# GpSimd's preparation of RWKV's first pass in pieces that wait for VectorE's units, and the two scans at the in-projection's end

## The reference, cut to what matters

```python
def block(q_blk):
    s = jnp.einsum('bhcqd,bhckd->bhcqk', q_blk, kt).astype(f32)
    pr = jax.nn.softmax(s, axis=-1)
    pd = pr[:, :, 0] - lam * pr[:, :, 1]
    return jnp.einsum('bhqk,bhkv->bhqv', pd.astype(vt.dtype), vt)
```

```python
w_log = -jax.nn.softplus(-(w0 + jnp.einsum('bsdr,drc->bsdc', jnp.tanh(wd), w2))) - 0.5
decay = jnp.exp(-jnp.exp(w_log))
a = jax.nn.sigmoid(a0 + jnp.einsum('bsdr,drc->bsdc', ad, a2))
kk = kk / jnp.maximum(jnp.sqrt(jnp.sum(kk * kk, axis=-1, keepdims=True)), 1e-12)
k_dir = k * (1.0 + (a - 1.0) * k_a)
```

## Time and profile before

| | |
|---|---|
| median of 3 runs | 1949.75 us (1945.37 to 1950.09) |
| the profiled execution | 1950.11 us, span 1948.4 us |
| busy: TensorE / VectorE / ScalarE / GpSimd | 95% / 57% / 36% / 11% |
| mean granted TensorE clock | 0.984 of full speed |
| last tile of the in-projection taken out | 1092.41 |
| VectorE's first reduction of the attention | 1097.02 |
| VectorE's first instruction of RWKV's heads | 1153.37 |

### The profile page before, as it was taken

One profiled execution on the slowest core, in us unless ns is written; L12 is line 12 of the kernel. 1 busy time (PEld: TensorE's weight loads), 2 busy tenths in 40 slices (PEclk: granted clock), 3 DMA queues, 4 the chain that ended last, 5 costly groups with the idle time before them and its releaser, 6 DMA issues. The chain is left out here.

```text
span 1948.4 us, 35667 instructions
## 1 busy us (share of the span) xinstructions
PE 1860.3 (95%) x15284; PEld 1489.4 (76%) x15284; DVE 1106.2 (57%) x1648; ACT 693.0 (36%) x1154; POOL 222.0 (11%) x217
## 2 busy tenths in 40 slices
PE   8999999999998999999999789989999999999996
PEld 6887758688886666778888568878868888888875
DVE  4664354553266777443467787777565635354444
ACT  4325332341223787432222373333223312122342
POOL 4210011140002000210111240000001000000011
PEclk9999999999999999989999899999989999999998
DMA  5334323152223000224331100001042232323121
GB/s 186 114 109 141 139 73 108 44 226 79 86 70 121 12 34 2 71 90 154 115 113 33 47 2 4 3 3 50 23 173 87 98 108 87 108 87 103 60 98 43
DMA packets 42379, 160.73 MB, mean 82 GB/s; under 512 B 4976, under 2 KB 14192, under 8 KB 27632
## 3 DMA queue, kind: packets, MB, share of 16 engines
q1 hardware_dynamic: 28016, 143.78, 21.5%
q10 hardware_dynamic: 14208, 14.68, 2.1%
HBM read 140.36 MB, written 16.78 MB: 81 GB/s over the span
## 5 line engine op out<-in xcount | busy, mean ns | idle before, releaser
L257 DVE TENSOR_TENSOR wlo<-raw,whi 128x2048 fp32r<-128x2048 f32 (+2 forms) x113 | 251.4, 2226 | 184.0 <-ACT whi L248 183.8
L248 ACT ACTIVATE whi<-raw 128x2048 fp32r<-128x2048 f32 (+2 forms) x113 | 209.0, 1850 | 318.1 <-PE ps L283 161.4
L281 PE MATMUL ps<-act_hi,whi 128*128 128x512 f32 x616 | 243.5, 395 | 0.0
L301 PE MATMUL ps<-act_lo,whi 128*128 128x512 f32 x632 | 242.7, 394 | 0.0
L283 PE MATMUL ps<-act_hi,wlo 128*128 128x512 f32 x616 | 240.7, 391 | 0.0
L282 PE MATMUL ps<-act_lo,whi 128*128 128x512 f32 x616 | 240.6, 391 | 0.0
L300 PE MATMUL ps<-act_hi,whi 128*128 128x512 f32 x592 | 235.6, 398 | 0.0
L305 PE MATMUL ps<-act_hi,wlo 128*128 128x512 f32 x632 | 157.2, 391 | 0.0
L301 PEld LDWEIGHTS ps<-act_lo,whi 128*128 128x128 f32 x632 | 120.0, 190 | 25.7 <-issue 1.2
L305 PEld LDWEIGHTS ps<-act_hi,wlo 128*128 128x128 f32 x632 | 119.3, 189 | 25.0
L300 PEld LDWEIGHTS ps<-act_hi,whi 128*128 128x128 f32 x592 | 111.1, 188 | 32.3 <-issue 8.1
(11 more groups left out here) (520 smaller groups left out, 3381.3 us busy)
## 6 DMA issues: line engine op xcount, KB each, us to landing
raw<-stream_in SPq DMA_DIRECT2D x107, 1024.0 KB, 4.8
v_scratch<-v_out ACTq DMA_DIRECT2D x16, 256.0 KB, 3.4
z_scratch<-zt ACTq DMA_DIRECT2D x16, 256.0 KB, 3.0
mlh_v<-v_scratch SPq DMA_DIRECT2D x4, 1024.0 KB, 4.8
mlh_z<-z_scratch SPq DMA_DIRECT2D x16, 256.0 KB, 2.6
cmp_w<-cmp_w_in SPq DMA_DIRECT2D x2, 2048.0 KB, 11.2
z_scratch<-in_zt ACTq DMA_DIRECT2D x16, 256.0 KB, 2.1
mix_g<-z_scratch SPq DMA_DIRECT2D x16, 256.0 KB, 6.1
```

What stands on the lines that cost most here:

```text
L248: act.activation(k.whi[b % 2][:, 0:n], k.raw[b % RAW_SLOTS][:, 0:n], ACT.Copy).then_inc(k.hi_done, 1)
L257: dve.tensor_tensor(k.wlo[b % 2][:, 0:n], k.raw[b % RAW_SLOTS][:, 0:n], k.whi[b % 2][:, 0:n].bitcast(F32), ALU.subtract).then_inc(k.lo_don ...
L281: pe.matmul(bank, hi, x_hi, start=(x == 0), stop=False)
L301: pe.matmul(bank, hi, x_lo, start=False, stop=False)
```

## The change

Five things are done.

1. `rw_b` waits for the last tile but one, not for the last.
2. The scans stand in `stage_in_2` before VectorE's wait for the last tile. X and E1 swap places in memory for that (X at 104, E1 at 100), and the copies of `rhs` by ScalarE wait accordingly one step earlier. ScalarE's two pairs of sigmoids are issued in the passes of the last two tiles and wait for `lo_done` of a lower count.
3. GpSimd's instructions on both directions are split into one for each.
4. E1, E2 and X wait for neg_lam (`lam`); all later pieces wait besides for `pd_done` of a given count (`beside(m)`: m pairs done): `rw_rate` 1, `rw_kd` 2 and 3, the eight features 4 to 11, `rw_kds` 12, the two `rw_kh` 13 and 14.
5. ScalarE's exponentials come in passes 3 to 7.

```diff
@@ stage_in_2, ScalarE @@
+                if t >= K0 + RW_ALL - 2:
+                    m = t - K0 - RW_ALL + 2
+                    act.wait_ge(k.lo_done, b1 - 2)
+                    rw_sigmoids(k, act, 0, m, (4 + 2 * m, 5 + 2 * m))
...
-            act.wait_ge(k.lo_done, b1)
-            rw_sigmoids(k, act, 0, 0, (4, 5))
-            rw_sigmoids(k, act, 0, 1, (6, 7))
@@ stage_in_2, VectorE @@
+                if t == K0 + RW_ALL - 1:
+                    dve.wait_ge(k.scan_landed, 16)
+                    rw_scans(k, dve, 0)
                 dve.wait_ge(k.tile_done, tile + 1)
@@ stage_da_attention, GpSimd @@
-            pool.wait_ge(k.tile_done, TILE_AT[b1])
+            def beside(m):
+
+                pool.wait_ge(s["pd_done"], m)
+
+            pool.wait_ge(k.tile_done, TILE_AT[b1 - 1])
             pool.wait_ge(k.dap["kkn"], RW_T)
-            past(pool, "sigs", 4)
-            pool.tensor_tensor(bb[:], both(kkn), rate[:], ALU.mult).then_inc(ss["bb"], 1)
+            for d in range(2):
+                past(pool, "sigs", 3 + d)
+                last = pool.tensor_tensor(bb[:, d, :], kkn, rate[:, d, :], ALU.mult)
+            last.then_inc(ss["bb"], 1)
+            pool.wait_ge(k.dap["lam"], 1)
             past(pool, "scan", 2)
-            pool.tensor_tensor(E1[:], X[:], sig[:], ALU.subtract).then_inc(ss["e1"], 1)
+            for d in range(2):
+                last = pool.tensor_tensor(E1[:, d, :], X[:, d, :], sig[:, d, :], ALU.subtract)
+            last.then_inc(ss["e1"], 1)
...
+            beside(1)
+            for d in range(2):
+                last = pool.tensor_scalar(rate[:, d, :], rate[:, d, :], k.col("k_a"), omk, ALU.mult, ALU.add)
...
+            for d in range(2):
+                beside(2 + d)
+                last = pool.tensor_tensor(kd[:, d, :], rate[:, d, :], keys, ALU.mult)
...
-            pool.tensor_tensor(k.rw_kds[:], kd[:, 0, :], kd[:, 1, :], ALU.add).then_inc(ss["kds"], 1)
-            past(pool, "kds", 1)
             past(pool, "sums", 1)
             for d in range(2):
                 past(pool, "exps", 4 * d + 2)
                 past(pool, "pend", d + 1)
                 x = ar[:, d, 1, :]
+                beside(4 * d + 4)
                 pool.tensor_tensor(x, k.rw[:, 0, :], x, ALU.mult).then_inc(ss["feat"], 1)
+                beside(4 * d + 5)
...
+            beside(12)
+            pool.tensor_tensor(k.rw_kds[:], kd[:, 0, :], kd[:, 1, :], ALU.add).then_inc(ss["kds"], 1)
...
+                beside(13 + d)
+                pool.tensor_tensor(kh[:, d, :], kd[:, d, :], (E2, E1)[d][:, d, :], ALU.mult).then_inc(ss["feat"], 2)
@@ stage_da_attention, ScalarE @@
-                if 6 <= n < 11:
+                if 3 <= n < 8:
                     past(act, "sums", 1)
-                    exponentials[2 * (n - 6)]()
-                    exponentials[2 * (n - 6) + 1]()
+                    exponentials[2 * (n - 3)]()
+                    exponentials[2 * (n - 3) + 1]()
@@ stage_da_attention, VectorE @@
-                if n == 1:
-                    dve.wait_ge(k.scan_landed, 16)
-                    rw_scans(k, dve, 0)
@@ rw_tensors @@
-    first = [k.at(f"rw_first_{n}", [P, 2, S], F32, at) for n, at in (("X", 100), ("E1", 104), ("E2", 84), ("sig", 76))]
+    first = [k.at(f"rw_first_{n}", [P, 2, S], F32, at) for n, at in (("X", 104), ("E1", 100), ("E2", 84), ("sig", 76))]
@@ stage_rw_heads, ScalarE @@
-                if c == 0 and n in (0, 4):
-                    past(act, "feat", c, (10, 12)[n // 4])
-                    act.wait_ge(daa["bh"], n // 4 + 1)
+                if c == 0 and n in (0, 3):
+                    past(act, "feat", c, (10, 12)[n // 3])
+                    act.wait_ge(daa["bh"], n // 3 + 1)
```

More of the change, by code:

```diff
@@ L2273, in _ @@
             kkn, keys = k.kkn[:, 0, :], k.rw[:, 4, :]
-            def both(x):
-                return x.rearrange("p (o n) -> p o n", o=1).to_broadcast([P, 2, S])
             pool.tensor_scalar(omk, k.col("k_a"), -1.0, 1.0, ALU.mult, ALU.add).then_inc(s["omk"], 1)
             pool.tensor_scalar(k.da_scale, k.col("subln"), 1.0 - LAMBDA_INIT, None, ALU.mult).then_inc(s["omk"], 1)
-            pool.wait_ge(k.tile_done, TILE_AT[b1])
+            def beside(m):
+                pool.wait_ge(s["pd_done"], m)
+            pool.wait_ge(k.tile_done, TILE_AT[b1 - 1])
             pool.wait_ge(k.dap["kkn"], RW_T)
-            past(pool, "sigs", 4)
-            pool.tensor_tensor(bb[:], both(kkn), rate[:], ALU.mult).then_inc(ss["bb"], 1)
+            for d in range(2):
[3 more added lines that the diff above has]
+            pool.wait_ge(k.dap["lam"], 1)
             past(pool, "scan", 2)
-            pool.tensor_tensor(E1[:], X[:], sig[:], ALU.subtract).then_inc(ss["e1"], 1)
+            for d in range(2):
+                last = pool.tensor_tensor(E1[:, d, :], X[:, d, :], sig[:, d, :], ALU.subtract)
+            last.then_inc(ss["e1"], 1)
             for d in range(2):
@@ L2295, in _ @@
             pool.wait_ge(s["omk"], 2)
-            pool.tensor_scalar(rate[:], rate[:], k.col("k_a"), omk, ALU.mult, ALU.add).then_inc(ss["kdt"], 1)
+            beside(1)
+            for d in range(2):
+                last = pool.tensor_scalar(rate[:, d, :], rate[:, d, :], k.col("k_a"), omk, ALU.mult, ALU.add)
+            last.then_inc(ss["kdt"], 1)
             past(pool, "kdt", 1)
             pool.wait_ge(k.rw_done, RW_ALL)
-            pool.tensor_tensor(kd[:], rate[:], both(keys), ALU.mult).then_inc(ss["kd"], 1)
+            for d in range(2):
+                beside(2 + d)
+                last = pool.tensor_tensor(kd[:, d, :], rate[:, d, :], keys, ALU.mult)
+            last.then_inc(ss["kd"], 1)
             past(pool, "kd", 1)
-            pool.tensor_tensor(k.rw_kds[:], kd[:, 0, :], kd[:, 1, :], ALU.add).then_inc(ss["kds"], 1)
-            past(pool, "kds", 1)
             past(pool, "sums", 1)
@@ L2307, in _ @@
                 x = ar[:, d, 1, :]
+                beside(4 * d + 4)
                 pool.tensor_tensor(x, k.rw[:, 0, :], x, ALU.mult).then_inc(ss["feat"], 1)
+                beside(4 * d + 5)
                 pool.tensor_tensor(ar[:, d, 0, :], kkn, (E1, E2)[d][:, d, :], ALU.mult).then_inc(ss["feat"], 1)
                 past(pool, "exps", 4 * d + 3)
+                beside(4 * d + 6)
                 pool.tensor_tensor(bt[:, d, :], bb[:, d, :], X[:, d, :], ALU.mult).then_inc(ss["feat"], 1)
+                beside(4 * d + 7)
                 pool.tensor_tensor(kt[:, d, :], kd[:, d, :], X[:, d, :], ALU.mult).then_inc(ss["feat"], 1)
+            beside(12)
+            pool.tensor_tensor(k.rw_kds[:], kd[:, 0, :], kd[:, 1, :], ALU.add).then_inc(ss["kds"], 1)
+            past(pool, "kds", 1)
             past(pool, "feat", 8)
@@ L2315, in _ @@
                 past(pool, "exps", 4 * d + 4)
-                e = (E2, E1)[d][:, d, :]
-                pool.tensor_tensor(kh[:, d, :], kd[:, d, :], e, ALU.mult).then_inc(ss["feat"], 2)
+                beside(13 + d)
+                pool.tensor_tensor(kh[:, d, :], kd[:, d, :], (E2, E1)[d][:, d, :], ALU.mult).then_inc(ss["feat"], 2)
         @block.scalar
```

## The result

The changed kernel takes 1935.05 us (median of 6 runs, 1933.01 to 1937.38) against 1949.22 of the kernel before, measured beside it (6 runs, 1945.37 to 1952.39). The ratio is 0.9934, with a 95% interval of 0.9923 to 0.9944: 12.9 us less (10.9 to 15.0), where the two medians by themselves are 14.2 apart. Measured again (experiment 10) it is 0.9944 (0.993 to 0.9957), 10.9 us less. The forecast was 1942.5 and its range ended at 1938.5: right in sign, the gain half again to three quarters larger than forecast, and the time outside the range. On the chip of experiments 1 to 4 one further launch of the kernel before took 4713.9 us; it is left out of the figures there.

The account below looks back on a forecast made before the run. VectorE was taken to set the pace in the differential attention, though TensorE is busy 95% of the span. Terms -1.28 - 1.75 + 0.2 - 9.3 + 3.6 + 1.1 = -7.4 gave 1942.5 us, range 1938.5 to 1948.5.

Parts of the forecast that it names:

- (e): TensorE in the differential attention: clock falls to 1.2 GHz, VectorE waits for the first two products; 3.6 us lost.
- (a): rw_b leaves the last tile's evacuation, so VectorE's L2158 falls from 1.77 to 0.49: 1.28 us saved.
- (b): The two scans move into VectorE's idle time before the last tile: net 1.75 us saved, 0.2 spilled over.
- (c): VectorE's pairs (L2377, L2379) avoid GpSimd's paced pieces: 9.3 of 11.7 us of stalls saved, 2.4 left in the opening.
- (f): ScalarE's exponentials move to n = 3..7, making Exps late around units 8 to 10: 1.1 us lost.
- rival 2: GpSimd's pieces start 0.2 late and meet the next L2377: 8.5 us could return, in practice 1948; chance 0.12.
- rival 3: ScalarE and TensorE take over the pace in the middle of the stage: 1945.3; chance 0.16.
- Rival 1: TensorE's clock does not fall at the stage's start, that loss shrinking from 3.6 to 1.2: 1940.1; chance 0.18.
- Rival 4: TensorE stays at 1.2 GHz through the stage: +13 us, 1963; chance 0.04.

Follow-up runs that it names:

- experiment 10: The changed kernel measured again, unaltered: 1938.18 us (5 runs), ratio 0.9944 to the kernel before.
- experiment 1: Kernel before with only early scans and rw_b (X and E1 swapped, sigmoids moved); GpSimd whole, no pair waits, exponentials at n = 6: 1940.18 us, ratio 0.9964.
- e2: Changed kernel without GpSimd's waits for finished pairs (pd_done), all else kept: 1942.2 us (7 runs), ratio 0.9972.
- e3: Changed kernel with ScalarE's exponentials back in passes 6 to 10: 1937.91 us (4 runs), ratio 0.9946.
- e7: Changed kernel with TensorE's scores 4 to 7, turns 1 to 5 and products 0 to 4 done twice: 1943.76 us (one execution).
- e11: Changed kernel with GpSimd's awaited pair counts from 4 on one higher: 1936.2 us (6 runs), ratio 0.9935.
- e12: Changed kernel with the opening paced too (rw_rate behind rw_b, E2 and X one per unit, later pieces two pairs later, exponentials at n = 4): 1936.37 us, 0.9941.
- e4: Kernel before with only the exponentials moved to passes 3 to 7: 1947.38 us (10 runs), ratio 1.0001.
- e8: Kernel before with TensorE's scores 4 to 7, turns 1 to 5 and products 0 to 4 done twice: 1955.61 us (one execution).
- e9: Kernel before with two filler matmuls in TensorE's gaps, before and behind the first turns: 1947.55 us (one execution).
- e6: Kernel before with five 128x512 filler matmuls behind the first two sets of scores, to hold the clock up: 1952.76 us (one execution).
- experiment 5: Changed kernel with four 128x512 filler matmuls behind the first two sets of scores, to hold the clock up: 1938.23 us (one execution).

## Why the prediction was wrong, step by step

The sign was right, and so was where the gain comes from (the terms a to c). The one wrong term is the loss (e). The terms against what the two profiles show:

| step | forecast | measured | from |
|---|---|---|---|
| (a) L2158 without `rw_b` | -1.28 | -1.30 | first reduction after `in_u`: 4.61, 3.31 |
| (b) scans out of the loop | -1.75 | -1.77 | reciprocal after first reduction: 4.51, 2.74 |
| (b) spilled over | +0.2 | 0 | `in_u` starts 0.11 after the next scores (0.17 before) |
| (c) stalls | -9.3 | -8.7 | 11.7 less 3.0 |
| (e), (f) TensorE and ScalarE late | +4.7 | +0.6 | the remainder, see below |
| sum | -7.4 | -11.2 | 60.96, 49.72 |

**(a) and (b)** hold. The early `rw_b` did hold VectorE, but in its idle time: the last instruction of the tile before (L2165 at 1083.25) took 1.66 instead of 0.75, and the scans 3.31 instead of 2.33. They ended at 1088.25, just as the tile came.

**(c)** holds within 0.6, but not piece by piece, and 2.0 of it came with the early scans and not with the waits (experiment 1). I had put the opening's leftovers at 2.4; they are 0.38, 0.74, 0.42 and 0.38 (1.9), and the fifth is ScalarE's late `rw_pend`, which I had not seen: 1.04. The window of 1.49 with a piece of 1.26 has room indeed; rival 2 (pieces miss it) did not come true: from 1108.09 on no pair is stalled.

**(e) is the step that failed**: +3.6 forecast for matmuls at 1.2 GHz that `da_o` would wait for, and no such wait in the profile. That the clock falls was right, to 0.1 us (6.6 behind `in_u`, forecast 6.5). "I take it that the clock falls all the same" was followed by a return at 1112.8 read off the kernel before (its row's mean of 0.76 gives 1112.5). On the forecast's own clock (4.1 later) the changed kernel was back at 1102.4, 10 us sooner, before the scores of unit 4 that I had priced at half clock were even issued. What TensorE did in between differs. In before come scores, a gap of 2.08, four turns, a gap of 1.50, scores; the gaps were VectorE's stalls of 2.35 and more, passed on. The turns, of the profile of before:

```profile
1105.64 1.12 PE L2253 MATMUL ps<-consts,da_p 128*128 128x128 f32 x4 [2.08 <-DVE da_p L2379]
```

In after, the scores of 1094.34 and the turns of 1097.68 run without a gap, since the first pair is done at 1096.65, while TensorE is still in those scores. I had shortened the stalls of the first pair in (c) and kept in (e) the low clock of a kernel that had them whole.

How far do the runs bear this out? With the scans early, that is with a short first pair, the low clock lasted 3.4 us in all eight executions that had no filler (after, e1, e2, e3, e7, e10, e11, e12), wherever it began between 5.8 and 7.1 us behind `in_u`. With the old opening it was low for 13.7, 13.7, 10.2 and 10.2 us in the stage (before, e4, e8, e9) and, held up at first, still for 6.8 (e6), behind a gap that the stalls left. That fits the stalls as the reason. But e8 had a first fall of 3.4 us with all its stalls, and paid the rest in a second fall; so what goes with the stalls is the low-clock time of the whole stage, and how it is divided changes from execution to execution. Why e8 came back early and before did not is open. What the low clock costs is shown more firmly: the 3.4 us left cost nothing (experiment 5), though they do cost a wait of 0.94 once the opening has no stalls (experiment 12), and slow matmuls in the middle would have cost about what (e) said for a unit (experiment 7).

The prediction had weighed the Trainium skill's "TensorE: Matmul & The Clock Gate", section "What's actually happening": activity lifts the throttled state. The traces agree with its direction: the clock came back within dense work in before (1112.5), after (1098.3), e8 (1099.9) and e9 (1099.7). I had given it 0.8 us of (e) where all 3.6 went, because I let the dense work start at 1104.0 of my clock and not with the scores at 1098.5.

**(f)**, +1.1 forecast, is in the same +0.6: VectorE's idle time before `da_o` rose from 2.05 to 2.27 us, and the other 0.4 I put down to starts a few hundredths late at TensorE's pace of 2.54. ScalarE did become the pace for a while, as rival 3 said: TensorE's scores start 2.94, 3.14, 2.74 and 3.15 apart from 1104.85 to 1116.82, and wait for ScalarE's Exp, while ScalarE itself shows no idle time there. But in the same units VectorE has its stall of 1.04, so one covers the other; experiment 11 took the stall and gained nothing. And experiment 3 shows that the price has the other sign: exponentials at their old place cost 1.77.

Rival 1 (1940.1) was the nearest in time, and for the wrong reason: the idle time was short as it said (4.14), but the clock did fall. Rival 4 (slower) had nothing in its favour. The range was too narrow below because its lower end took (e) at 1.2 and the stalls a little better than forecast, when (e) at nothing was possible: -1.28 - 1.75 - 9.3 = -12.3 makes 1950.1 - 12.3 = 1937.8, already below the range's 1938.5. The stage's 11.24 alone make 1949.22 - 11.24 = 1938.0 of the median; that it came out at 1935.05 is 2.9 us that the stage doesn't explain; launches of one kernel spread over more than that (4.4 and 7.0 us in these two sixes), and the second measurement's gain was the smaller 10.9.

Not tried: why the low-clock time ahead of the stage is 10 us in one execution and 20 in another of the same kernel. It moves a launch by some 4 us and stays open.

## What to carry to other kernels

A state read off the trace of before, such as the length of a low clock, can be part of what the stalls produced, and one trace doesn't show how much it varies: when the change removes the stalls, redo that timeline too, and don't keep its length. Work beside a bottleneck engine can be paced by that engine's own count of finished units, one piece per unit and placed beside an instruction that it doesn't hold back (here the reduction from PSUM); it holds only for pieces whose data are there by then, and the last units have no room. Once the stalls of one engine are down to a few tenths a unit, look for the engine next to it before removing more: here two further versions took away stalls of 1.0 and 3.0 us, brought 0.9 back at the end and gained nothing that shows.
